# Sixteen modulation steps leave a ten-step recurrence for the input units ahead of it; scores are multiplied anew, three weight splits come after it

## The chip, the cores and the metric

The kernel runs on one core of one Trainium2 chip. The metric is the time of one execution in microseconds (us) on the device; lower is better. Engines are named as in the profile: PE (TensorE matmul), DVE (VectorE), ACT (ScalarE), POOL (GpSimd), SP (SyncE, which here only issues DMAs; its issue instructions are shown as SPq).

## The reference

The kernel computes one inference step of a two-layer backbone in fp32 for 128 context tokens and 512 latent tokens (640 in all, width 1024). Each layer is: half-step SwiGLU FFN, token mixing, half-step SwiGLU FFN. The even layer mixes by neighbourhood attention and by an mLSTM, the odd one by a gated short convolution.

```python
def modulation(cond, w, b):
    m = jax.nn.silu(cond) @ w + b
    return m.reshape(cond.shape[0], 1, N_MOD, D_MODEL)
def modulate_in(x, g_pre, mod, j):
    return rmsnorm(x, g_pre) * (1.0 + mod[:, :, 3 * j + 1]) + mod[:, :, 3 * j]
def gated_residual(x, out, g_post, mod, j, weight):
    return x + weight * mod[:, :, 3 * j + 2] * rmsnorm(out, g_post)
```

The change is about two parts of it. One is `modulation`: for each layer the two conditioning vectors times a 1024 x 9216 weight, that is 9 parts of 1024 columns. The other is the mLSTM of the even layer: 4 heads of width 128, in chunks of 128 tokens, two directions. Each of its 10 steps (5 chunks, 2 directions) takes scores (queries times keys), weights them by a decay, multiplies them with the values, adds the queries times the running memory C, and updates C.

## The kernel before, in words

The six sublayers (`SUBS`) run one after the other: ffn, ab (attention and mLSTM), ffn, ffn, sc (convolution), ffn. Every weight tile is loaded by SP into one of two slots `w_raw`, copied by ACT to `w_hi` (L1455), and DVE subtracts the copy to get `w_lo` (L2023); PE then multiplies hi by hi, lo by hi and hi by lo. Load n waits until tile n-2 is split.

**Modulation parts.** Most parts are summed by DVE from `ada_tile` rows (`mod_acc`, L2207 to L2209). Five parts (`DIRECT`, in sublayers 0, 1, 2, 3; sublayer 1 has two) go over PE instead: `load_direct` (L666) loads a 128x1024 piece of 512 KB into one of four slots `ada_direct`, and `direct_step` (L1086) multiplies it by the conditioning, 4 matmuls per piece (L1098) and 8 pieces per part, with 4 matmuls for the bias ahead of the first (L1096). `direct_out` (L1579) copies the sums to SBUF on ACT, `store_direct` (L688) stores them. SP issues all these loads and stores. In the FFN sublayers four steps stand behind unit 3 and four behind unit 5. The 16 steps of sublayer 1 stand inside the recurrence, two or three behind each of its steps 2 to 8 (`REC_AT`), with their loads between those of the output weight (`REC_LOADS`).

**The ab sublayer** has 23 input units (a 128-column tile of the input weight times all tokens, L1321, some 7.0 us each; unit 3 is a narrow one with the gates), with attention between the later ones. Then comes the recurrence: `products(q)` (L1337) multiplies the scores of step q, `back(q)` multiplies numerators (L1372, L1374) and the state's update (L1382). Around it, per step: POOL makes `q_scaled` (L1982), `v_weighted` (L1995) and a masked `decay` (L1973); ACT takes two exponentials (L1791, L1835); DVE makes `scoresT` (L2598) and finishes the step with denominators, `h_sum` and `C_state` (L2600 to L2629). Queries and keys of a chunk give the same product in both directions, so the scores of steps 0, 1, 2 are copied to SBUF by ACT (`keep_scores`, L1838) and used again in steps 7, 6, 5 (`SCORE_KEPT`). Splits of output weight tiles 1, 2, 3 stand on ACT and DVE behind steps 1, 3, 5.

**The output projection** of ab has 8 tiles of the contraction (15 matmuls of 128x512 each). Tiles 0 to 2 need only attention's output; then `turn_heads` transposes the normalised heads, and tiles 3 to 7 follow. SP's queue behind the recurrence: four stores of the final state, a wait for their landing (`st_out`), `load_gate`, output weight tiles 6 and 7, the stores of the two direct parts, the reload of x from DRAM (5 x 512 KB), the modulation columns of the next sublayer (`load_cols`), and the other weight loads.

## Time and profile before

| | |
|---|---|
| median of 3 runs | 2472.9 us (2469.79 to 2474.32) |
| the profiled execution | 2478.73 us, span 2476.8 us, mean granted clock 0.993 |
| ab sublayer: input units from | 502 us |
| the recurrence, first to last step on PE | 774.5 to 827.8 us |
| busy over the span | PE 98%, DVE 71%, ACT 40%, POOL 17% |

The span is that of one execution taken by the profiler. A row of the timeline gives the start, the duration, the engine, the line, the operation, the tile written and those read, and how many were joined (x4). What stands in brackets is how long the engine stood idle ahead of it and what it waited for. PE runs at one of two clock levels (1.2 and 2.4 GHz); a granted clock (PEclk) of 1.00 is the upper one. Matmuls overlap, so the distance between the starts of two rows tells more than their durations.

### The profile page before, as it was taken

How to read it: one execution, taken by the hardware profiler on the slowest of the kernel's cores; microseconds unless marked ns; L12 is line 12 of the kernel's file. 1: busy time of each engine (PE TensorE's matmuls, PEld its weight loads, DVE VectorE, ACT ScalarE, POOL GpSimd, SP SyncE). 2: the span in 40 equal slices, each digit the busy share in tenths (PEclk: the TensorE clock that was granted, in tenths of full speed). 3: DMA queues.
4: the chain of work that ended last, by engine and by line, in shares of the span. 5: the costliest groups of instructions: out<-in, count | busy, mean ns of one | idle time of the engine just before them, and what ended most of it. 6: DMA issues, size and time to landing. Idle time of an engine off the chain costs nothing. (4 is left out here: it accounts for less than half of the span.)

```text
span 2476.8 us, 39028 instructions
## 1 busy us (share of the span) xinstructions
PE 2416.2 (98%) x15205; PEld 2210.2 (89%) x15205; DVE 1747.8 (71%) x2449; ACT 983.4 (40%) x1924; POOL 411.8 (17%) x410
## 2 busy tenths in 40 slices
PE   6999999999998999999999999999999999999998
PEld 6997998889887789979988997999899979989997
DVE  5978785666555668778855988686567459866864
ACT  4442443532444454424435442343421154423432
POOL 1120220201214122102203220121200022201211
PEclk9999999999999999999999999999999999999999
DMA  8426334174124534263343426333244323243333
GB/s 260 129 61 219 100 87 139 54 232 111 46 58 164 186 112 131 80 207 86 86 162 112 124 72 209 98 86 115 90 145 137 103 85 103 69 149 99 86 110 112
DMA packets 346646, 297.95 MB, mean 120 GB/s; under 512 B 38219, under 2 KB 296251, under 8 KB 346464
## 3 DMA queue, kind: packets, MB, share of 16 engines
q1 hardware_dynamic: 346464, 295.46, 39.3%
q8 instruction: 122, 2.00, 0.3%
q14 instruction: 60, 0.49, 0.1%
HBM read 280.57 MB, written 14.80 MB: 119 GB/s over the span
## 5 line engine op out<-in xcount | busy, mean ns | idle before, releaser
L2023 DVE TENSOR_TENSOR w_lo<-w_raw,w_hi 128x512 fp32r<-128x512 f32 (+1 forms) x249 | 218.9, 882 | 254.7 <-ACT w_hi L1455 253.3
L1455 ACT ACTIVATE w_hi<-w_raw 128x512 fp32r<-128x512 f32 (+1 forms) x249 | 188.1, 760 | 473.7 <-DMA w_raw<-in_ffn_w_dram 205.5
L949 PE MATMUL psum<-w_hi,act_hi 128*128 128x512 f32 x800 | 319.0, 399 | 2.3 <-DVE w_lo L2023 2.1
L951 PE MATMUL psum<-w_hi,act_lo 128*128 128x512 f32 x800 | 317.1, 396 | 0.0
L950 PE MATMUL psum<-w_lo,act_hi 128*128 128x512 f32 x800 | 317.0, 396 | 0.0
L1082 PE MATMUL psum<-hT_hi,w_hi 128*128 128x320 f32 x912 | 281.9, 309 | 0.5 <-DVE z_quarters L2309 0.5
L1083 PE MATMUL psum<-hT_lo,w_hi 128*128 128x320 f32 x912 | 281.8, 309 | 0.0
L1084 PE MATMUL psum<-hT_hi,w_lo 128*128 128x320 f32 x912 | 281.8, 309 | 0.0
L949 PEld LDWEIGHTS psum<-w_hi,act_hi 128*128 128x128 f32 x800 | 150.6, 188 | 44.0 <-DVE w_lo L2023 5.5
L1082 PE MATMUL psum<-t_hi,w_hi_more 128*128 128x320 f32 x608 | 187.9, 309 | 0.0
L1084 PE MATMUL psum<-t_hi,w_lo_more 128*128 128x320 f32 x608 | 187.9, 309 | 0.0
L1083 PE MATMUL psum<-t_lo,w_hi_more 128*128 128x320 f32 x608 | 187.8, 309 | 0.0
L1932 POOL TENSOR_TENSOR w_sum<-w_raw 128x512 f32<-128x512 f32 x36 | 55.2, 1534 | 783.2 <-DVE w_lo L2271 783.2
L951 PEld LDWEIGHTS psum<-w_hi,act_lo 128*128 128x128 f32 x800 | 150.6, 188 | 36.6
L950 PEld LDWEIGHTS psum<-w_lo,act_hi 128*128 128x128 f32 x800 | 150.7, 188 | 35.4
L1082 PEld LDWEIGHTS psum<-hT_hi,w_hi 128*128 128x128 f32 x912 | 171.2, 188 | 0.7 <-DVE w_lo_more L2271 0.7
L1083 PEld LDWEIGHTS psum<-hT_lo,w_hi 128*128 128x128 f32 x912 | 171.2, 188 | 0.0
L1084 PEld LDWEIGHTS psum<-hT_hi,w_lo 128*128 128x128 f32 x912 | 171.2, 188 | 0.0
L1036 PE MATMUL psum<-hT_hi,w_hi 128*128 128x320 f32 x608 | 140.2, 312 | 2.4 <-DVE w_lo L2023 2.3
L1036 PE MATMUL psum<-hT_hi,w_lo 128*128 128x320 f32 x608 | 138.5, 309 | 0.0
L1036 PE MATMUL psum<-hT_lo,w_hi 128*128 128x320 f32 x608 | 138.4, 309 | 0.0
L2325 DVE TENSOR_TENSOR z_quarters<-z_quarters 128x640 f32<-128x640 f32 x76 | 127.4, 1676 | 4.8 <-ACT z_quarters L1624 4.8
(303 smaller groups left out, 5906.0 us busy)
## 6 DMA issues: line engine op xcount, KB each, us to landing
w_raw<-in_ffn_w_dram SPq DMA_DIRECT2D x96, 512.0 KB, 4.5
w_raw_next<-in_ffn_w_dram SPq DMA_DIRECT2D x80, 512.0 KB, 5.4
w_raw<-in_ffn_w_dram SPq DMA_DIRECT2D x148, 256.0 KB, 3.0
ada_tile_ffn<-in_ada_w_dram SPq DMA_DIRECT2D x56, 512.0 KB, 4.5
ada_direct<-in_ada_w_dram SPq DMA_DIRECT2D x40, 512.0 KB, 6.0
w_raw<-in_ab_w_in_dram SPq DMA_DIRECT2D x28, 512.0 KB, 4.3
w_raw<-in_sc_w_in_dram SPq DMA_DIRECT2D x24, 512.0 KB, 4.0
x_kept_rows<-x SPq DMA_DIRECT2D x20, 512.0 KB, 5.7
```

Of the source, the lines that this page charges most:

```text
L949: mm(out, a_hi, b_hi, start=first, stop=False)
L950: mm(out, a_hi, b_lo, start=False, stop=False)
L951: return mm(out, a_lo, b_hi, start=False, stop=final)
L1036: last = mm(IN[p][0:width, h, 0:HT], a, b[:, k, h * HT:(h + 1) * HT], start=(k == 0 and a is hi and b is hT_hi), stop=(k == KD - 1 and a i ...
L1082: mm(out, hi[:, k, :], o_hi[:, k, :], start=(k == 0 and q < 4), stop=False, **on)
L1083: mm(out, hi[:, k, :], o_lo[:, k, :], start=False, stop=False, **on)
L1084: last = mm(out, lo[:, k, :], o_hi[:, k, :], start=False, stop=(k == KH - 1), **on)
L1455: A(dst, src, ACT.Copy).then_inc(w_hi_ok, 1)
L1932: pool.tensor_tensor(S1[:], A21(g), A22(g), ALU.add).then_inc(ws_ok, 1)
L2023: V.tensor_tensor(d_, a, b.bitcast(F32), ALU.subtract).then_inc(w_lo_ok, 1)
L2325: V.tensor_tensor(Z[:, 2:4, :], Z[:, 0:2, :], Z[:, 2:4, :], ALU.mult).then_inc(q_summed, 1)
```

## The change

1. The 16 direct steps of sublayer 1 leave the recurrence: two stand behind each of the input units 3, 4, 5, 6, 8, 9, 10 and 11 (`AB_AT`), in PSUM bank 5. ACT copies the rows of the two parts behind units 7 and 11 (`AB_ROWS`) instead of behind the recurrence.
2. All loads and stores of direct parts, those of the FFN sublayers too, are issued by POOL instead of SP: in an FFN sublayer behind POOL's two `t_sum` additions, in ab at POOL's start.
3. `keep_scores` is gone; the scores of steps 5, 6 and 7 are multiplied anew (`SCORE_STEPS`), in alternating banks.
4. DVE splits the output weight tiles 1, 2, 3 behind the recurrence, between the scalings of heads; ACT's split of tile 3 comes behind it too.
5. The reload of x is issued behind input unit 15, and `load_cols` comes ahead of output weight tile 6.

```diff
-REC_AT = {2: (0, 2), 3: (2, 5), 4: (5, 8), 5: (8, 10), 6: (10, 12), 7: (12, 14), 8: (14, 16)}
-REC_LOADS = {3: (4, 8), 4: (8, 10), 5: (10, 16)}
+AB_AT = {u: range(2 * i, 2 * i + 2) for i, u in enumerate((3, 4, 5, 6, 8, 9, 10, 11))}
+AB_ROWS = {7: 0, 11: 1}
...
# SP
+                            if u == 15:
+                                direct_done(sp, s, 1, KD - 1)
+                                for t in range(NT):
+                                    reload_x(s, t)
...
-                        load_out(s, ab_w_out[0], 0, ph, 1, 3)
-                        for k in range(4):
-                            load_direct(s, 0, k)
-                        for u in range(3, AB_SPLIT):
-                            load_out(s, ab_w_out[0], 0, ph, u, u + 1)
-                            for j in range(*REC_LOADS[u]):
-                                load_direct(s, j // KD, j % KD)
+                        load_out(s, ab_w_out[0], 0, ph, 1, AB_SPLIT)
...
                         load_gate(s)
-                        load_out(s, ab_w_out[0], 0, ph, AB_SPLIT, AB_SPLIT + 2)
-                        for z in range(2):
-                            store_direct(s, z)
-                        for t in range(NT):
-                            reload_x(s, t)
-                        sp.wait_ge(mod_stored, STORED(DB[s] + 1))
                         load_cols(s + 1)
-                        load_out(s, ab_w_out[0], 0, ph, AB_SPLIT + 2)
+                        load_out(s, ab_w_out[0], 0, ph, AB_SPLIT)
...
# PE
                     modulation(ph, u)
+                    for j in AB_AT.get(u, ()):
+                        direct_step(1, j // KD, j % KD)
...
-                    if q in (2, 3):
+                    if q >= 2:
                         pe.wait_ge(ml_st, q - 1)
-                        pe.wait_ge(sc_kept, q - 1)
...
                     if q + 2 in SCORE_STEPS:
                         products(q + 2)
-                    if q == 2:
-                        pe.wait_ge(ml_st, 3)
-                        pe.wait_ge(sc_kept, 3)
-                    for j in range(*REC_AT.get(q, (0,))):
-                        direct_step(1, j // KD, j % KD)
...
# POOL, ffn
+                    for k in range(KD) if s in DIRECT else ():
+                        load_direct(s, 0, k)
...
# POOL, ab
+                    for j in range(2 * KD):
+                        load_direct(s, j // KD, j % KD)
+                        if j == KD + 3:
+                            store_direct(s, 0)
+                    store_direct(s, 1)
...
# DVE
-                    if q in (1, 3, 5):
-                        split(ph["nout"] + (q + 1) // 2, shape="out", u=(q + 1) // 2)
                 for n in range(2, NT):
+                    split(ph["nout"] + n - 1, shape="out", u=n - 1)
                     head_scale(n)
...
-SCORE_STEPS = [0, 1, 2, 3, 8]
-SCORE_BANK = {0: 0, 1: 1, 2: 0, 3: 1, 4: 1, 8: 1, 9: 1}
-SCORE_KEPT = {5: 2, 6: 1, 7: 0}
+SCORE_STEPS = [0, 1, 2, 3, 5, 6, 7, 8]
+SCORE_BANK = {0: 0, 1: 1, 2: 0, 3: 1, 4: 1, 5: 0, 6: 1, 7: 0, 8: 1, 9: 1}
```

Behind step 3 of the recurrence PE has this before: the state's update, three direct steps (pieces 2, 3 and 4 of the first part), the numerators of step 4.

```order
L1382 MATMUL psum<-v_weighted,km_tok 128x129 x3
L1098 MATMUL psum<-ada_direct_150,cond_silu 2x256 [waits direct_loaded2]
L1098 MATMUL psum<-ada_direct_150,cond_silu 2x256 x3
L1098 MATMUL psum<-ada_direct_151,cond_silu 2x256 [waits direct_loaded3]
L1098 MATMUL psum<-ada_direct_151,cond_silu 2x256 x3
L1098 MATMUL psum<-ada_direct_148,cond_silu 2x256 [waits direct_loaded0]
L1098 MATMUL psum<-ada_direct_148,cond_silu 2x256 x3
L1372 MATMUL psum<-vm_tok,scoresT 128x129 [waits ml_h,ml_cs,ml_qs,ml_st]
```

In the change four products of scores for step 5 stand there instead, and the bias with the first two steps now stands ahead of the narrow input unit with the gates (the unit's first matmul is the last row but one; it waits for its own split):

```order
L1054 MATMUL psum<-direct_bias_161,pick 2x256 [waits direct_loaded0]
L1054 MATMUL psum<-direct_bias_161,pick 2x256 x3
L1056 MATMUL psum<-ada_direct_148,cond_silu 2x256 x4
L1056 MATMUL psum<-ada_direct_149,cond_silu 2x256 [waits direct_loaded1]
L1056 MATMUL psum<-ada_direct_149,cond_silu 2x256 x3
L1280 MATMUL psum<-hT_hi,w_hi 16x320 [waits in_evac1,w_lo_ok]
L1280 MATMUL psum<-hT_hi,w_hi 16x320
```

So PE's queue now meets the landing of these pieces in the input units, and no longer in the recurrence.

At the end of the recurrence DVE has this before (the copy of the last state, three head scalings, the splits of tiles 4 and 5):

```order
L2628 COPY C_state<-psum 128x516 [waits ml_c]
L2637 TENSOR_TENSOR h_sum<-h_sum,h_r 128x512 [waits h_r_ok] x3
L2023 TENSOR_TENSOR w_lo<-w_raw,w_hi 128x512 [waits w_hi_ok] x2
```

and in the change (the splits of tiles 1, 2 and 3 between the scalings):

```order
L2609 COPY C_state<-psum 128x516 [waits ml_c]
L2006 TENSOR_TENSOR w_lo<-w_raw,w_hi 128x512 [waits w_hi_ok]
L2618 TENSOR_TENSOR h_sum<-h_sum,h_r 128x512 [waits h_r_ok]
L2006 TENSOR_TENSOR w_lo<-w_raw,w_hi 128x512 [waits w_hi_ok]
L2618 TENSOR_TENSOR h_sum<-h_sum,h_r 128x512 [waits h_r_ok]
L2006 TENSOR_TENSOR w_lo<-w_raw,w_hi 128x512 [waits w_hi_ok]
L2618 TENSOR_TENSOR h_sum<-h_sum,h_r 128x512 [waits h_r_ok]
L2006 TENSOR_TENSOR w_lo<-w_raw,w_hi 128x512 [waits w_hi_ok] x2
```

SP's queue in the change, from the loads of output tiles 3, 4 and 5 on (each waits for the split of the tile two before it):

```order
L594 DMA w_raw<-in_ab_w_out_dram 128x512 [waits w_lo_ok] x3
L594 DMA held_ab_raw_115<-in_ab_w_out_dram 128x512
L594 DMA w_raw<-in_ab_w_out_dram 128x512 [waits w_lo_ok]
L594 DMA held_ab_raw_118<-in_ab_w_out_dram 128x512
L594 DMA w_raw<-in_ab_w_out_dram 128x512 [waits w_lo_ok]
L594 DMA held_ab_raw_121<-in_ab_w_out_dram 128x512
L594 DMA out_dram<-C_state 128x4x128 [waits ml_cs]
L594 DMA out_dram<-C_state 128x4x1
L594 DMA out_dram<-C_state 128x4x128 [waits ml_cs]
L594 DMA out_dram<-C_state 128x4x1
L594 DMA gate<-modulation 128x2x1024 [waits direct_stored,mod_stored,x_new,ml_h,st_out]
```

The stores of the state stood behind the same loads before too, but those loads waited for splits inside the recurrence. POOL, in the third sublayer of the change:

```order
L1900 TENSOR_TENSOR t_sum_189<-hT_hi,hT_lo 128x1280
L1879 DMA direct_bias_162<-in_ada_b_dram 1x16x64 [waits xT_ok]
L1881 DMA ada_direct_152<-in_ada_w_dram 128x1024
L1881 DMA ada_direct_153<-in_ada_w_dram 128x1024 [waits xT_ok]
L1881 DMA ada_direct_154<-in_ada_w_dram 128x1024 [waits xT_ok]
L1881 DMA ada_direct_155<-in_ada_w_dram 128x1024 [waits xT_ok]
L1881 DMA ada_direct_152<-in_ada_w_dram 128x1024 [waits direct_used]
```

Before, SP issued these loads ahead of `t_sum`; now they follow it on POOL.

## Rows read from the trace of the kernel before

**Rows 1.** The page: busy time over the span

```profile
PE 2416.2 (98%) x15205; PEld 2210.2 (89%) x15205; DVE 1747.8 (71%) x2449; ACT 983.4 (40%) x1924; POOL 411.8 (17%) x410
```

**Rows 2.** Waits of PE, 771 to 862 us: in total, times, longest

```profile
PE psum L1098 <- DMA ada_direct<-in_ada_w_dram: 6.9, 4, 5.8
PE psum L1372 <- DVE scoresT L2598: 6.2, 2, 4.6
```

**Rows 3.** Timeline of PE in the recurrence (start us, us, engine, line, operation)

```profile
774.51 0.46 PE L1372 MATMUL psum<-vm_tok,scoresT 128*128 128x129 f32 x2 [1.56 <-DVE scoresT L2598]
...
777.27 1.06 PE L1351 MATMUL psum<-featT 128*128 128x128 f32 x8
...
778.16 0.39 PE L1372 MATMUL psum<-vm_tok,scoresT 128*128 128x129 f32 x2
...
782.70 0.46 PE L1372 MATMUL psum<-vm_tok,scoresT 128*128 128x129 f32 x2 [0.47 <-issue]
...
791.73 0.80 PE L1372 MATMUL psum<-vm_tok,scoresT 128*128 128x129 f32 x2 [4.60 <-DVE scoresT L2598]
...
815.99 1.03 PE L1098 MATMUL psum<-ada_direct,cond_silu 128*2 128x256 f32 x8 [5.76 <-DMA ada_direct<-in_ada_w_dram]
...
827.82 0.48 PE L949 MATMUL psum<-w_hi,mix_act 128*128 128x512 f32 x1
```

**Rows 4.** Timeline of DVE in the recurrence

```profile
783.72 7.35 DVE L2023 TENSOR_TENSOR w_lo<-w_raw,w_hi 128x512 fp32r<-128x512 f32 x1 [1.22 <-ACT w_hi L1455]
...
798.15 1.76 DVE L2598 TENSOR_TENSOR scoresT<-scores_kept,decay 128x512 f32<-128x512 f32 x1
```

**Rows 5.** Timeline of POOL in the recurrence

```profile
781.31 1.28 POOL L1982 TENSOR_TENSOR q_scaled<-featT,w_inter 128x512 f32<-128x512 f32 x1
...
784.79 1.28 POOL L1982 TENSOR_TENSOR q_scaled<-featT,w_inter 128x512 f32<-128x512 f32 x1
```

**Rows 6.** Busy time by engine in the recurrence (core 0: us, PE, PEld, DVE, ACT, POOL, PEclk, DMA)

```profile
771.00:828.00 57.00, 43.44 (x395) 34.21 (x394) 37.19 (x91) 29.60 (x108) 33.87 (x32) 0.91 0.65 221
```

**Rows 7.** Timeline of SP behind the recurrence

```profile
826.35 4.37 SPq L606 DMA_DIRECT2D out_dram<-C_state  x4
...
838.87 0.37 SPq L606 DMA_DIRECT2D gate<-modulation  x1
...
839.79 0.43 SPq L606 DMA_DIRECT2D w_raw<-in_ab_w_out_dram  x1
```

**Rows 8.** Timeline of ACT, output tile 6

```profile
846.15 0.63 ACT L1455 ACTIVATE w_hi<-w_raw 128x512 fp32r<-128x512 f32 x1 [10.09 <-DMA w_raw<-in_ab_w_out_dram]
```

**Rows 9.** Timeline of DVE, output tile 6

```profile
850.62 0.69 DVE L2023 TENSOR_TENSOR w_lo<-w_raw,w_hi 128x512 fp32r<-128x512 f32 x1
```

**Rows 10.** Timeline of PE, output tile 6

```profile
851.38 0.50 PE L949 MATMUL psum<-w_hi,mix_act 128*128 128x512 f32 x1
```

**Rows 11.** Timeline of PE in the ab input units

```profile
519.62 0.46 PE L1321 MATMUL psum<-hT_hi,w_hi 128*16 128x320 f32 x2 [2.44 <-DVE w_lo L2023]
...
591.38 1.89 PE L1117 MATMUL psum<-mod_acc_ab,pick 128*2 128x256 f32 x16 [3.75 <-DVE mod_acc_ab L2209]
...
594.43 0.73 PE L1321 MATMUL psum<-hT_hi,w_lo 128*128 128x320 f32 x2
```

**Rows 12.** A stretch of the ab input units (columns as in Rows 6, then GB/s)

```profile
515.00:525.00 10.00, 7.56 (x52) 5.44 (x52) 9.30 (x10) 1.88 (x4) 0.00 (x0) 1.00 1.00 301
```

**Rows 13.** Timeline of POOL, third sublayer

```profile
913.74 6.16 POOL L1926 TENSOR_TENSOR t_sum<-hT_hi,hT_lo 128x1280 f32<-128x1280 f32 x2 [15.32 <-DVE w_lo L2023]
```

**Rows 14.** Timeline of PE, third sublayer

```profile
929.01 0.61 PE L1096 MATMUL psum<-direct_bias,pick 1*2 1x256 f32 x8
...
929.54 1.91 PE L1098 MATMUL psum<-ada_direct,cond_silu 128*2 128x256 f32 x32
```

**Rows 15.** A stretch of the third sublayer (columns as in Rows 6)

```profile
920.00:930.00 10.00, 10.00 (x81) 8.91 (x83) 9.93 (x8) 5.36 (x6) 0.00 (x0) 1.00 0.19 55
```

**Rows 16.** The page: DMA issues, median us to landing

```profile
ada_direct<-in_ada_w_dram SPq DMA_DIRECT2D x40, 512.0 KB, 6.0
```

More of the change, by code:

```diff
@@ L14 @@
-import itertools
 from contextlib import ExitStack, contextmanager
@@ L343, in build @@
             [where["silu_g"], where["u_tmp"], a3] + [hh + i * 2048 for i in range(5)] + [hl + i * 2048 for i in range(2)])]
-        Sk = [at(f"scores_kept{i}", [P, MLH, P], hl + 4096 + i * 2048) for i in range(3)]
         hssq = at("h_ssq", [P, NT * MLH], hl + half + 8192 + 480)
@@ L461, in build @@
             ph[-1]["mods_end"] = mb
-            if s == 1:
-                DB[s], mb = mb, mb + len(DIRECT[s])
         parts = [(s, z) for s in DIRECT for z in range(len(DIRECT[s]))]
-        direct_parts = [DB[s] + z for s, z in parts]
-        bias_until = list(itertools.accumulate(16 if b in direct_parts else 64 for b in range(mb)))
         held_use = lambda s, i: (1 if i < NT else 0) + sum(1 for q in range(s + 1) if plan[q][-1]["held"] > i)
@@ L733, in load_pairs @@
                         keep_x(s, t)
-                    for k in DIRECT_LOADS.get(2 * i + 1, ()) if s in DIRECT else ():
-                        load_direct(s, 0, k)
                 for g in range(ph["g0"], ph["g1"]):
@@ L1098, in direct_step @@
                     last = mm(out(i), csil[:, :, k], direct[s][k % 4][:, cols(i)], start=False, stop=(k == KD - 1))
-                last.then_inc(mod_mm if k == KD - 1 else direct_used, 1)
+                last.then_inc(direct_used, 1)
             def modulation(ph, u):
@@ L1174, in out_phase @@
                         turns({3: (0, 1), 4: (2,), 5: (3,)}[k])
-                    for t in ((0, 1, NT - 1, 2, 3) if ph.get("ab") and k == 0 else range(NT)):
+                    for t in ((NT - 1, 0, 1, 2, 3) if ph.get("ab") and k == 0 else range(NT)):
                         if k == 0:
@@ L1856, in mixing @@
                     if n == NT - 1:
-                        direct_out(1, 0)
-                        direct_out(1, 1)
+                        split(ph["nout"] + 3, shape="out", u=3)
                     head_squares(n)
```

138 lines of the change are left out of this document (65 added, 73 removed).

## The prediction, made before the change had run

> **What bounds the kernel now.** The page first: PE is busy 98% of the span [rows 1], so almost every microsecond that PE is spared or kept waiting counts, and work of other engines is free as long as PE does not wait for it. Then I looked for PE's waits around the recurrence [rows 2]: 6.9 us for the landing of direct pieces and 6.2 us for `scoresT`. The timeline of PE shows where they are [rows 3]. The recurrence runs from 774.51 to 827.82, that is 53.3 us for ten steps. Its second step begins 3.65 us after its first, and that is what a step of PE costs with numerators, state update and four score products (the products are the 0.9 us from 777.27 to 778.16). Ten such steps would be 36 us. What lies between is three things: 16 direct steps; an idle of 4.60 us ahead of step 3, and one of 5.76 us ahead of a direct step; and the lower clock level after them, since the granted clock is 0.91 over the stretch [rows 6].
>
> The first idle is not a lack of DVE time. DVE's split of an output tile, which takes 0.69 us elsewhere [rows 9], took 7.35 us there, and `scoresT` stood behind it [rows 4]. POOL worked back to back in this time, starting a scaled query every 3.48 us [rows 5]. So a DVE instruction with two SBUF operands was held for as long as POOL kept going; a `scoresT` that reads `scores_kept` from SBUF was stretched as well, to 1.76 us [rows 4]. The Trainium skill, "SBUF — State Buffer", section "Who interferes with whom", says that a DVE operation with two SBUF inputs and a GpSimd operation that reads SBUF exclude each other for one whole instruction. The trace agrees on the direction and not on the size, as 7.35 us is several POOL instructions of 1.28 us and not one.
>
> **(a) The recurrence without direct steps, splits and kept scores.** It removes 16 steps, both idles and both clock drops, and adds three groups of products at 0.9 us. POOL sets the pace at first: step 2 can begin no earlier than before, 782.70, because its scaled query ends at 782.59 [rows 3, 5]. Step 3 follows 3.48 us later (784.79 + 1.28 us, 786.2 with the signal). From there PE's own 3.65 us is the longer period: steps 4, 5 and 6 begin at 789.8, 793.4 and 797.0. DVE is no bound: of its 37.19 us over the stretch [rows 6] some 9.4 are splits, so 2.8 us a step. Steps 6 and 7 have no state update (2.7 and 1.8 us); 8 and 9 alternate with DVE at about 2.5 us each. The end comes at 806.6 instead of 827.82: **-21.2 us, I take -21**. If POOL and DVE alternate less well it is -19.5; I see no way past -21.5. The three copies of scores taken from ACT save nothing by themselves.
>
> **(b) The 16 steps in the input units.** A step is 1.91 / 4 = 0.48 us by the row and 0.46 by the starts, a bias 0.53 [rows 14]. The first two steps and their bias (1.5 us) stand ahead of the gates' unit, where PE idles 2.44 us anyway for a split that waits behind `mod_acc` on DVE [rows 11]. They fit into the gap, but they must have landed, and in this stretch the 16 DMA engines are busy all the time (share 1.00, 301 GB/s) [rows 12] with the weight and `ada_tile` loads on which that split depends: 2 MB more at 301 GB/s is 7 us of such traffic. Between nothing and 7 us I take +1.9 for the gates' unit and +1 for later landings. The other 14 steps and the second bias are 14 x 0.46 + 0.53 = 7.0, with 0.1 for each change between streams 7.7. Against it stands the wait of 3.75 us at 591.38 for a `mod_acc` [rows 11]. The work that leads to it starts from the turned context gates, behind unit 9; only the four steps of units 10 and 11 come into the wait and fill it, -1.9. With 1.9 us of idle left the clock should stay up, as it did at the 2.44 us idle [rows 11, 12], and the stretch after 591.38, where a pair of 128x320 matmuls takes 0.73 instead of 0.46 us [rows 11], goes: -2.4 over some 5 us. ACT's row copies, moved into its idle time behind units 7 and 11, cost nothing; POOL has no work before unit 13. Sum 1.9 + 1 + 7.7 - 1.9 - 2.4: **+6.3**, between +3.5 (no late landing) and +10 (late tiles and the clock drop kept).
>
> **(c) The tail.** Let T be the start of the output projection (827.82 before). SP must issue the loads of tiles 3, 4, 5 and then four stores; it waits for their landing, and only then come gate, columns and tile 6. Before, the stores were issued from 826.35 to 830.72, T+2.9 at the last; the gate went out at T+11.05, so 8.15 us for landing [rows 7]. Now load 3 waits for the split of tile 1, which DVE makes after its last state copy at T+1.9; load 5 waits for the split of tile 3, which waits for load 3 to land: T+8.3. The stores go at T+9.1 to T+11.1 and have landed at T+19.3. Gate, g_post and three column loads take 2.2 us, so load 6 is issued at T+21.5. Before, ACT's copy of tile 6 began 6.36 us after its load [rows 7, 8] and took 0.63 us; add DVE's 0.69 and tile 6 is ready at T+29.2. PE came to it at T+23.56 without a wait, just after the split's end at 851.31 [rows 9, 10]. So **a new wait of +5.7 us**, and as after the idles of 3.75 to 5.76 us above, a stretch at the lower level, +1.7: **+7.4**, between 0 (stores landing in 3 us because nothing else is under way, loads too) and +10 (the head scalings, between which the splits now stand, late as well). The direct rows' stores and the reload of x, which leave this place, were hidden there behind other work and give nothing.
>
> **(d) The FFN sublayers.** POOL ends `t_sum` at 919.90 [rows 13] and PE wants the bias at 929.01 [rows 14]: 9.1 us for five issues and a landing. No row of this trace shows a DMA issued by POOL. From below: SP's issues, 0.43 us for a weight tile [rows 7], which with the 6.0 us of a landing [rows 16] give 8.2 us, no wait. From above: POOL is held like DVE was in [rows 4], DVE being busy 9.93 of 10 us here [rows 15]; five issues at 2 us plus a landing are 16 us, minus 9.1, less the 1.9 us that PE spends on the bias and the pieces ahead of the last: 5 us, three times. I take the lower end with a little, 0.3 us each, **+1**, because the DMA engines have room (share 0.19) [rows 15] and `t_sum` itself ran at its usual pace beside the same DVE work (3.1 us for 1280 columns [rows 13] against 1.28 for 512 [rows 5]). For the other four pieces PE is a unit pair later, and they have time.
> The Trainium skill, "DMA: Bandwidth & Descriptors", section "Anatomy of one DMA — SWDGE (gpsimd) path", gives 2.0 us plus bytes / 436e3 for a DMA issued by GpSimd; my estimate from it for one piece is 3.2 us, and that would leave no wait in (d).
>
> **Sum:** -21 + 6.3 + 7.4 + 1 = -6.3 us. Against the profiled execution, 2478.7, that is 2472.4; that execution lies 5.8 us above the median of 2472.9, so the forecast of the median is 2466.6, rounded **2467 us**.
>
> **The rivals.** A measurement of this kernel can tell 0.2%, 4.9 us, from no change: below 2468.0 is faster, above 2477.8 slower.
> *POOL's loads come late (the other side).* Mechanism: in three FFN sublayers, five issues of POOL, one after the other beside a busy DVE, last longer than the room behind `t_sum`. It decides from the point where an issue costs over about 1 us (5 x 1 + 6.0 - 1.9 = 9.1). At 2 us PE waits 4.5 to 5 us three times, with lower clock after it: +14 in place of +1, so **2480**. For it: DVE's 7.35 us shows that the two engines can hold each other for long, and DVE is never idle there. Against: `t_sum` is not stretched.
> The same section of "SBUF — State Buffer" in the Trainium skill has a warning by a box on DMAs of GpSimd, that DVE's two-port work starves the writing of their descriptors, 620 ns becoming 3100 ns; no run here shows it yet.
> *Late pieces in ab.* The 8 MB in input units land behind the weights in a stretch at share 1.00, and (b) is +12: **2473**, no change. For it: a piece took 6.0 us to land already where the engines were less busy [rows 6, 16]. Against: the pieces behind the first four are asked for a unit or more before their use.
> *The recurrence stays slow.* If the long hold of DVE came from POOL's pace and hits another operation, `h_sum` or `C_state` with their SBUF operands, 7 us come back: **2474**. Against: both read PSUM as well, and the two stretched instructions read SBUF alone [rows 4].
> *The tail has no new wait.* Stores that land in 3 to 4 us because the traffic of the direct pieces is gone take (c) to 0: **2459**.
>
> **How the numbers follow.** The forecast 0.45; POOL's loads late 0.15; late pieces in ab 0.15; recurrence slow 0.10; no wait in the tail 0.15. The forecast's own range, from its bounds, is 2461 to 2473, of which 0.32 of the 0.45 lies below 2468.0. Faster: 0.32 + 0.15 and a little of the others, 0.50. Same: the rest of the forecast, the two cases at 2473 and 2474, 0.33. Slower: POOL's loads and a part of late pieces, 0.17. The range 2459 to 2479 leaves out most of the 0.15 of the first rival and the far end of the last.
>
> **What would show it.** The recurrence on PE shorter by 21 us, with no idle over 1.6 us and no clock drop; in the units, PE 7 to 10 us more between unit 3 and the recurrence and the wait for `mod_acc` under 2.4 us; in the tail, a wait of 5 to 6 us for the split of tile 6, and the gate issued some 19 us behind T; in sublayers 0, 2 and 3 the bias matmul waiting under 1 us. The forecast is wrong if PE waits for `ada_direct` by several us in any sublayer, if a step of the recurrence takes over 4 us, or if tile 6 is not waited for.

## The result, and the profile after

| | before | changed |
|---|---|---|
| median (20 runs each, the same chip) | 2471.64 us | 2476.42 us |
| lowest to highest | 2468.05 to 2477.3 us | 2472.71 to 2481.76 us |
| the profiled execution | 2478.73 us | 2474.26 us |

The ratio is 1.0017, with an interval of 1.0011 to 1.0023: the changed kernel is slower by 4.2 us. That is under the 0.2% that the prediction took as its bound, so the verdict is "same". The forecast was 2467, 5 us faster; the direction was wrong, and the time lies inside the range. Note the third line: the profiled execution of the changed kernel is 4.5 us *shorter* than that of before. What a reader of these two traces alone would conclude is the opposite of what the medians say, and a part of this study is about that.

The page of the changed kernel:

```profile
span 2472.5 us, 39072 instructions
PE 2414.1 (98%) x15229; PEld 2208.0 (89%) x15229; DVE 1739.1 (70%) x2449; ACT 983.5 (40%) x1921; POOL 444.1 (18%) x475
q0 software_dynamic: 6560, 21.04, 2.3%
ada_direct<-in_ada_w_dram POOLq DMA_DIRECT2D x40, 512.0 KB, 6.0
```

Nothing here tells where time went. POOL's queue now carries the 40 pieces, and they land as fast as before, 6.0 us in the median [rows 16].

**The recurrence** did what was asked of it. PE's timeline from its first step to the output projection:

```profile
785.10 0.46 PE L1330 MATMUL psum<-vm_tok,scoresT 128*128 128x129 f32 x2 [1.56 <-DVE scoresT L2579]
...
788.75 0.39 PE L1330 MATMUL psum<-vm_tok,scoresT 128*128 128x129 f32 x2
...
793.27 0.46 PE L1330 MATMUL psum<-vm_tok,scoresT 128*128 128x129 f32 x2 [0.46 <-issue]
...
817.36 0.48 PE L906 MATMUL psum<-w_hi,mix_act 128*128 128x512 f32 x1
```

From 785.10 to 817.36 it takes 32.26 us, against 53.31 [rows 3]: 21.05 us less, where 21 was forecast. Over this stretch the clock is up throughout, where it was 0.91 [rows 6]:

```profile
785.00:817.36 32.36, 29.84 (x257) 29.00 (x257) 25.13 (x83) 23.04 (x90) 31.37 (x32) 1.00 0.20 59
```

**The input units** are where it is given back. PE's waits between 483 and 785 us:

```profile
PE psum L1280 <- DVE w_lo L2006: 4.7, 2, 4.5
PE psum L1192 <- DVE probs L2451: 1.9, 1, 1.9
PE psum L1075 <- DVE mod_acc_ab L2194: 0.2, 1, 0.2
```

The wait for `mod_acc` that was 3.75 us [rows 11] is down to 0.2. But the gates' unit waits 4.51 us instead of 2.44 for its split, and there is a wait for `probs` that before did not have:

```profile
521.52 0.71 PE L1280 MATMUL psum<-hT_hi,w_hi 128*16 128x320 f32 x2 [4.51 <-DVE w_lo L2006]
...
628.80 0.55 PE L1192 MATMUL psum<-ident,probs 128*128 128x128 f32 x3 [1.92 <-DVE probs L2451]
```

The first of these durations is already the lower clock level at work (0.71 us, 0.46 in the kernel before [rows 11]). On DVE, the multiplication by the conditioning ahead of the gates' split stood 9.15 us for a load of `ada_tile`, where it had stood 5.54. Before, then changed:

```profile
515.37 1.42 DVE L2207 TENSOR_SCALAR mod_acc_ab<-ada_tile_ab,cond_silu 128x1024 f32<-128x1024 f32 x2 [5.54 <-DMA ada_tile_ab<-in_ada_w_dram]
...
517.27 1.42 DVE L2192 TENSOR_SCALAR mod_acc_ab<-ada_tile_ab,cond_silu 128x1024 f32<-128x1024 f32 x2 [9.15 <-DMA ada_tile_ab<-in_ada_w_dram]
```

The stretches there (us, then busy time of PE, PEld, DVE, ACT, POOL, then granted clock, DMA share and GB/s) show traffic in place of work, and the clock going down behind the wait:

```profile
505.00:515.00 10.00, 9.79 (x67) 9.53 (x66) 1.23 (x1) 1.89 (x4) 1.93 (x4) 1.00 0.99 307
515.00:525.00 10.00, 5.49 (x42) 2.52 (x41) 6.58 (x7) 2.08 (x5) 1.23 (x2) 0.78 1.05 383
525.00:535.00 10.00, 10.00 (x71) 6.71 (x70) 9.06 (x8) 1.64 (x2) 1.07 (x2) 0.88 1.04 281
```

A second execution of before has in the first two of them:

```profile
505.00:515.00 10.00, 9.62 (x66) 9.35 (x65) 1.23 (x1) 2.20 (x5) 0.00 (x0) 1.00 0.78 176
515.00:525.00 10.00, 7.52 (x52) 5.30 (x51) 8.24 (x9) 1.89 (x4) 0.00 (x0) 1.00 1.06 328
```

The four pieces asked for at POOL's start, from 504.76 us on, raise the traffic of the first stretch to 307 GB/s, from 176 here and 200 and 186 in the first and third executions of before. The loads that the gates' split hangs on land later; that the pieces are the cause is tested below (thin pieces).

**The tail** has the wait that was forecast. SP behind the recurrence, and then the ACT, DVE and PE rows of output tile 6:

```profile
825.67 2.44 SPq L594 DMA_DIRECT2D out_dram<-C_state  x4
837.51 0.37 SPq L594 DMA_DIRECT2D gate<-modulation  x1
...
840.17 0.44 SPq L594 DMA_DIRECT2D w_raw<-in_ab_w_out_dram  x1
```

```profile
845.22 0.63 ACT L1408 ACTIVATE w_hi<-w_raw 128x512 fp32r<-128x512 f32 x1 [15.28 <-DMA w_raw<-in_ab_w_out_dram]
845.88 0.69 DVE L2006 TENSOR_TENSOR w_lo<-w_raw,w_hi 128x512 fp32r<-128x512 f32 x1 [5.20 <-ACT w_hi L1408]
846.63 0.79 PE L906 MATMUL psum<-w_hi,mix_act 128*128 128x512 f32 x1 [5.34 <-DVE w_lo L2006]
```

**The FFN sublayers** show no wait: POOL issues its loads in 0.54 us each, and PE has no wait for a piece or a bias in any of them. In the third:

```profile
914.07 0.65 POOL L1879 DMA_DIRECT2D direct_bias<-in_ada_b_dram  x1
914.72 2.14 POOL L1881 DMA_DIRECT2D ada_direct<-in_ada_w_dram  x4
```

The two traces by stage, from the starts of the same PE rows, in us. The marks are the first product of input unit 0 (484.25 us before; the 502 us given ahead of the prediction is the start of unit 2), the first step of the recurrence, the output projection, output tile 6, and the transposes of the last of five token tiles of the new x. The last mark stands 7 to 10 us into the third sublayer's first products, so that what PE loses around them is counted in "ab".

| | input units | recurrence | to tile 6 | to the end of ab | ab |
|---|---|---|---|---|---|
| before | 290.3 | 53.3 | 23.6 | 53.0 | 420.1 |
| changed | 302.1 | 32.3 | 29.3 | 52.0 | 415.6 |

That is +11.8, -21.1, +5.7, -1.0: ab is 4.5 us shorter, and so are the profiled executions. The medians differ by 4.8 us the other way.

One statement ahead of the prediction needs mending: the narrow input unit with the gates is unit 4, counted from 0, not unit 3. The first two direct steps stand behind unit 3, ahead of it.

### The profile page after: what moved, and what is told of

The parts are those of the page before. It is cut to its first block and busy times, and to the rows that moved or that the text cites. A ratio compares the mean times of both kernels' runs of the same rounds, so it can differ in the third digit from the quotient of the medians.

```text
span 2472.5 us, 39072 instructions
## 1 busy us (share of the span) xinstructions
PE 2414.1 (98%) x15229; PEld 2208.0 (89%) x15229; DVE 1739.1 (70%) x2449; ACT 983.5 (40%) x1921; POOL 444.1 (18%) x475
## 5 line engine op out<-in xcount | busy, mean ns | idle before, releaser
L2006 DVE TENSOR_TENSOR w_lo<-w_raw,w_hi 128x512 fp32r<-128x512 f32 (+1 forms) x249 | 211.2, 851 | 270.0 <-ACT w_hi L1408 269.1
```

Source lines behind the costliest of these rows:

```text
L2006: V.tensor_tensor(d_, a, b.bitcast(F32), ALU.subtract).then_inc(w_lo_ok, 1)
```

## The experiments

Medians are in us; each ratio is to before, with its 95% interval, from runs of before on the same chip. Edits are made on the changed kernel, but for the last one, which is made on before.

**Both kernels again, unchanged.** Two more pairs were wanted to see what in the two traces is the kernel's and what is one execution's.

> The kernel before, unchanged. Theory 1: its first profiled execution (2478.7 us, above all its 20 timed runs) was an unlucky one, with a wait of 5.8 us for a direct piece, one of 4.6 us for scoresT and three drops of the clock. Another execution lies near 2471.6 us and its trace shows a recurrence of some 46 to 50 us instead of 53.3, or a drop of the clock less at 895 us. Rival: the execution looks as before, 53 us in the recurrence, and its place in time differs for reasons outside of these stretches. Ratio to the kernel before: 1.000.

> The changed kernel, unchanged. Theory 1: ratio 1.0017 (+4 us), recurrence 32.3 us, wait for output tile 6 of 5.3 us, input units 10 to 12 us longer than before, as in its first trace; of these the input units vary most, since their pieces compete with the weights. Rival: recurrence or tail vary by more than 1 us.

> The kernel before, a third profiled execution. Theory 1 (the 53.3 us of the first trace was the long end): recurrence of 47 to 51 us, split in the recurrence of 1 to 2 us and not 7.35, waits for direct pieces 5 to 9 us in sum. Rival: 53 us again. Input units 290 us in both.

> The changed kernel, a third profiled execution. If profiled executions of the changed kernel lie below its median by more than chance, this one does too, by 1 to 3 us, and its ab sublayer is 416 us from the first input unit to the end of the projection as in the other two. If it was chance, it is as likely above. Recurrence 32.3 us, input units 301 to 302 us.

| | median | ratio | profiled execution | units | recurrence | to tile 6 | to the end | ab |
|---|---|---|---|---|---|---|---|---|
| before again | 2474.29 | 1.0003 (0.9992 to 1.0014) | 2479.12 | 290.1 | 48.8 | 23.6 | 51.1 | 413.6 |
| before, third | 2474.57 | 0.9999 (0.9988 to 1.0010) | 2477.83 | 291.3 | 49.9 | 23.6 | 51.6 | 416.3 |
| changed again | 2480.39 | 1.0024 (1.0013 to 1.0035) | 2478.28 | 301.6 | 32.3 | 30.1 | 52.1 | 416.0 |
| changed, third | 2478.63 | 1.0026 (1.0017 to 1.0035) | 2479.92 | 303.9 | 32.3 | 29.6 | 52.4 | 418.1 |

Four things follow. First, the changed kernel is slower in each comparison, by 0.17, 0.24 and 0.26%. Second, its recurrence takes 32.3 us every time, while before's takes 53.3, 48.8 and 49.9 (the expected 46 to 50 for the second was right). The split of 7.35 us [rows 4] did not come back; the same split, then the product that reads kept scores, in the second execution of before:

```profile
783.57 1.65 DVE L2023 TENSOR_TENSOR w_lo<-w_raw,w_hi 128x512 fp32r<-128x512 f32 x1 [1.24 <-ACT w_hi L1455]
...
792.53 1.76 DVE L2598 TENSOR_TENSOR scoresT<-scores_kept,decay 128x512 f32<-128x512 f32 x1
```

What does come back each time is the wait for direct pieces, here 1.74 and 4.17 us ahead of two steps, and 5.9 us for the longest in the third execution. PE's timeline of the second and PE's waits of the third, from 774 to 862 us:

```profile
792.55 0.61 PE L1098 MATMUL psum<-ada_direct,cond_silu 128*2 128x256 f32 x8 [1.74 <-DMA ada_direct<-in_ada_w_dram]
...
810.07 0.62 PE L1098 MATMUL psum<-ada_direct,cond_silu 128*2 128x256 f32 x8 [4.17 <-DMA ada_direct<-in_ada_w_dram]
```

```profile
PE psum L1098 <- DMA ada_direct<-in_ada_w_dram: 9.0, 4, 5.9
```

Third, the means of three are -18.4 in the recurrence, +11.9 in the units, +6.1 to tile 6 and +0.3 behind it: in the traces ab comes out even (-0.1), outside ab nothing differs in a set way, and still the medians say +5.5. The gap sits in how the profiled executions lie to the medians: those of before lie 7.1, 4.8 and 3.3 us above the median of their own runs, those of the changed kernel -2.2, -2.1 and +1.3. The means are +5.1 and -1.0, 6 us apart, which is the gap.

Fourth, where before's excess sits is not settled. The first execution spends 4 us more in the recurrence than the other two. But the expectation that the second would lie near 2471.6 us was missed: its ab is 6.5 us shorter than the first's, and it is as long (2479.12 and 2478.73 us), because outside ab it takes 2063.6 us of its span against 2056.7. So single executions of one kernel scatter outside ab by more than the effect.

**Splits back in the recurrence.**

```diff
# ACT
-                    if q in (1, 3):
+                    if q in (1, 3, 5):
                         split(ph["nout"] + (q + 1) // 2, shape="out", u=(q + 1) // 2)
...
# DVE
+                    if q in (1, 3, 5):
+                        split(ph["nout"] + (q + 1) // 2, shape="out", u=(q + 1) // 2)
...
-                    split(ph["nout"] + n - 1, shape="out", u=n - 1)
```

> The changed kernel with the splits of output tiles 1, 2, 3 on DVE and ACT back inside the recurrence, behind steps 1, 3 and 5. Theory 1 (POOL working back to back holds a DVE instruction with two SBUF operands): one split takes 5 us or more and the recurrence gets 4 to 8 us longer, with a clock drop behind it; in return the loads of tiles 3 to 5 and the stores go out early and the wait for tile 6 (5.3 us and 1.7 us of lower clock) is gone: same time as the changed kernel within 3 us. Rival (the hold was an accident of one execution): splits of 0.7 to 1.3 us, recurrence 33 us, 7 us less than the changed kernel.

Measured: 2473.18, ratio 0.9998 (0.9986 to 1.0010); by the ratios some 6 us less than the changed kernel, where the rival had 7. The recurrence is 33.9 us, 1.6 longer, the way to tile 6 is 23.7, as before: the wait in the tail is gone. With direct steps out of the recurrence, splits inside it cost 0.88, 0.68 and 1.65 us, in DVE's timeline:

```profile
797.25 0.88 DVE L2004 TENSOR_TENSOR w_lo<-w_raw,w_hi 128x512 fp32r<-128x512 f32 x1 [0.76 <-ACT w_hi L1408]
...
812.80 1.65 DVE L2004 TENSOR_TENSOR w_lo<-w_raw,w_hi 128x512 fp32r<-128x512 f32 x1
```

The stores go out right behind the recurrence (the output projection starts at 822.36), and the gate 11.6 us behind that start, against 20.2 us in the changed kernel; PE's row of tile 6 has no wait:

```profile
821.36 4.37 SPq L594 DMA_DIRECT2D out_dram<-C_state  x4
...
833.95 0.37 SPq L594 DMA_DIRECT2D gate<-modulation  x1
```

```profile
846.07 0.48 PE L906 MATMUL psum<-w_hi,mix_act 128*128 128x512 f32 x1
```

So the split of three tiles behind the recurrence buys 1.6 us there and costs 5.9 us here.

**Stores ahead of the last load.**

```diff
-                        load_out(s, ab_w_out[0], 0, ph, 1, AB_SPLIT)
+                        load_out(s, ab_w_out[0], 0, ph, 1, 4)
...
+                        load_out(s, ab_w_out[0], 0, ph, 4, AB_SPLIT)
```

The four stores of the final state stand between the two.

> The changed kernel with one edit: the four stores of the final state are issued behind the load of output tile 3 and ahead of the loads of tiles 4 and 5. Theory 1 (the tail's wait hangs on when the stores land): the gate goes out some 4.5 us earlier, load 6 with it, PE's wait for tile 6 shrinks from 5.3 us to about 1 us and the clock does not drop: 6 us less than the changed kernel, ratio to the kernel before 0.9993. Rival (the landing of the stores is slow because of weight loads ahead of it, or load 6 is late for another reason): wait still over 3 us, ratio 1.001 or more.

Measured: 2481.26, ratio 1.0031 (1.0018 to 1.0043), a miss. The gate went out 19.6 us behind the projection's start instead of 20.2 and not 4.5 us earlier, and the wait moved forward and grew. PE, SP and ACT:

```profile
842.83 1.08 PE L1362 MATMUL psum<-ident,h_sum 128*128 128x128 f32 x4 [8.62 <-DVEq L2646]
```

```profile
822.14 3.12 SPq L594 DMA_DIRECT2D out_dram<-C_state  x4
825.30 1.12 SPq L594 DMA_DIRECT2D w_raw<-in_ab_w_out_dram  x1
```

```profile
838.01 0.63 ACT L1408 ACTIVATE w_hi<-w_raw 128x512 fp32r<-128x512 f32 x1 [7.90 <-DMA w_raw<-in_ab_w_out_dram]
```

The load of tile 4, issued behind the stores, was copied by ACT 12.7 us after its issue; DVE's split of it stands ahead of the last scalings of heads, and PE waited 8.6 us for those instead of 5.3 for tile 6. A split in an engine's program is a place where everything behind it waits for a DMA.

**Kept scores back** (on top of splits back): `keep_scores`, its semaphore and `SCORE_KEPT` as in the kernel before.

```diff
-SCORE_STEPS = [0, 1, 2, 3, 5, 6, 7, 8]
+SCORE_STEPS = [0, 1, 2, 3, 8]
+SCORE_KEPT = {5: 2, 6: 1, 7: 0}
```

> The changed kernel with the splits back in the recurrence and, in addition, the scores of steps 0 to 2 kept in SBUF by ACT and used again in steps 5 to 7, as in the kernel before (no scores multiplied anew). Theory 1 (the scores make no difference to the end of the recurrence by themselves: PE saves 3 x 0.9 us, but DVE's scoresT then reads two SBUF operands and is held beside POOL): recurrence 32 to 35 us, within 1.5 us of the 33.9 us with scores multiplied anew; two of three scoresT from kept scores take over 1.2 us. Rival (multiplying anew is a real cost on PE's path): recurrence 31.5 us or less and the kernel 2 us or more faster.

Measured: 2477.39, ratio 1.0010 (1.0001 to 1.0019), against 0.9998 for splits back alone. By the ratios it is 3 us slower, but the two intervals overlap, so the medians do not show it; the traces do for the recurrence. Neither expectation was met. The recurrence takes 37.2 us instead of 33.9, and PE's waits for `scoresT` grow from 2.5 to 6.5 us in total, the longest from 1.6 to 2.4:

```profile
PE psum L1335 <- DVE scoresT L2594: 6.5, 4, 2.4
```

```profile
805.01 1.75 DVE L2594 TENSOR_TENSOR scoresT<-scores_kept,decay 128x512 f32<-128x512 f32 x1
```

The three products that read kept scores take 1.75, 1.32 and 1.53 us where those that read PSUM take 0.68. Multiplying the scores anew, at 0.9 us of PE, gives the shorter recurrence once no direct step is in it.

**Direct steps one unit later.**

```diff
-AB_AT = {u: range(2 * i, 2 * i + 2) for i, u in enumerate((3, 4, 5, 6, 8, 9, 10, 11))}
+AB_AT = {u: range(2 * i, 2 * i + 2) for i, u in enumerate((4, 5, 6, 7, 8, 9, 10, 11))}
...
+                    pool.wait_ge(w_lo_ok, plan[s][0]["nin"] + 4)
```

The wait stands ahead of POOL's first load.

> The changed kernel with the direct steps of the ab sublayer one unit later: two behind each of units 4 to 11, and POOL issues the first load only once the gates' tile (unit 3) is split. Theory 1 (the 2 MB of the first four pieces land in a stretch where the DMA engines are full and delay ada_tile and with it the split of the gates' tile): PE's wait for the gates' unit falls from 4.2 to 4.5 us to the 2.4 us of the kernel before and the clock does not drop there; the input units get 4 to 6 us shorter, 296 to 298 us instead of 302. Rival (the two steps and their bias cost as much wherever they stand, or the pieces come too late for unit 4): input units 300 us or more, a wait for ada_direct.

Measured: 2478.31, ratio 1.0019 (1.0010 to 1.0028). The experiment missed its aim by one split: the wait let POOL go at 511.26 us, still ahead of the gates' unit, and that waited 4.46 us as in the changed kernel. The unit starts 37.4 us behind unit 0, against 38.4 to 38.8 in the three traces of the changed kernel and 34.7 to 35.4 in before's. So moving the two steps and the first loads gave back 1.2 us of 3.5; this run does not tell the steps from the loads. The units take 300.1 us, where the expectation had 296 to 298. That is 2.4 less than the changed kernel's mean, but stores early and splits back, which have its units unchanged, took 300.0 and 302.5.

**Loads later still.** The same with six units from unit 5 on and `nin + 5`.

```diff
+AB_AT = {5: range(0, 2), 6: range(2, 5), 7: range(5, 8), 8: range(8, 11), 9: range(11, 14), 10: range(14, 16)}
...
+                    pool.wait_ge(w_lo_ok, plan[s][0]["nin"] + 5)
```

> The changed kernel with the first direct loads of the ab sublayer issued only when the gates' tile is split (the run before let them go one split too early, while ada_tile was still landing), and with the 16 steps behind units 5 to 10, two or three each. Theory 1: PE's wait ahead of the gates is 2.4 us as in the kernel before and the clock stays up: gates' unit starts 35.3 us after the first unit, input units 3 to 6 us shorter than the changed kernel's 302, ratio 1.000 or 1.001. Rival: the wait stays over 4 us, or the traffic only moves the lateness to the weights of units 5 to 8 and the sum stays at 301 to 302 us.

Measured: 2480.82, ratio 1.0026 (1.0015 to 1.0037). Now the gates' unit waits 2.61 us with the clock up, as before; but the 16 pieces come in a denser row behind it, and a wait with a clock drop appears two units on:

```profile
519.10 0.46 PE L1280 MATMUL psum<-hT_hi,w_hi 128*16 128x320 f32 x2 [2.61 <-DVE w_lo L2007]
...
536.84 0.56 PE L1280 MATMUL psum<-hT_hi,w_hi 128*128 128x320 f32 x2 [2.03 <-DVE w_lo L2007]
```

The wait for `probs` is there as well (2.1 us). The units take 301.5 us against 302.5 in the mean: the lateness moved, it did not go, as the rival had it.

**The reload of x back in the tail.**

```diff
-                            if u == 15:
-                                direct_done(sp, s, 1, KD - 1)
-                                for t in range(NT):
-                                    reload_x(s, t)
...
+                        load_out(s, ab_w_out[0], 0, ph, AB_SPLIT, AB_SPLIT + 2)
+                        for t in range(NT):
+                            reload_x(s, t)
+                        load_out(s, ab_w_out[0], 0, ph, AB_SPLIT + 2)
```

> The changed kernel with the reload of x (5 x 512 KB) issued behind output tile 7 in the output phase, as before, instead of behind input unit 15. Theory 1 (the reload stands ahead of the input unit's weight load in SP's queue and in the DMA engines; ACT copies that weight 3.7 us late, DVE's split with it, and attention's probs behind the split): the wait of 1.5 to 2.2 us for probs near 629 us and its clock drop go, 3 to 5 us in the input units; nothing is lost in the tail. Rival (the wait has another cause, such as POOL's later bias additions): the wait stays and the input units are unchanged within 1 us.

Measured: 2479.33, ratio 1.0023 (1.0014 to 1.0032): no gain by itself. But the units take 298.7 us and the wait for `probs` is gone, and the reason is in SP's queue. In the changed kernel:

```profile
610.80 2.54 SPq L594 DMA_DIRECT2D x<-x_kept_rows  x5
613.38 7.06 SPq L594 DMA_DIRECT2D bias_raw<-bias_rep  x16
620.49 1.26 SPq L594 DMA_DIRECT2D w_raw<-in_ab_w_in_dram  x2
```

and with the reload late:

```profile
615.03 5.50 SPq L594 DMA_DIRECT2D bias_raw<-bias_rep  x16
620.57 1.26 SPq L594 DMA_DIRECT2D w_raw<-in_ab_w_in_dram  x2
```

By ACT's copy of a feature tile in the same unit (620.16 and 622.57 us), the weight load goes out 0.3 us behind it in the first and 2.0 us ahead of it in the second. ACT's copy of that weight, DVE's split and the softmax sums behind it all follow, and PE waits for their end. The size varies: the nine traces with the reload behind unit 15 have a wait for `probs` there of 0.3 to 2.3 us, the seven with the reload in the tail have none. In this execution some 4 us came back at 890 us, where the clock was 0.67 and 0.65 for 10 us. Six of the other 15 traces have a lower level between 880 and 905 us too (0.50 to 0.95 in two or three stretches of 5 us), the first and third of before among them, the rest not. It goes with no edit, so I read nothing into it, and the medians leave open whether the reload alone gains.

**Three repairs together** (splits back, steps one unit later, reload late), and the same with the later loads in place of the later steps.

> The changed kernel with three edits together: splits of output tiles 1 to 3 back in the recurrence, direct steps one unit later with late first loads, reload of x in the output phase. Theory 1: the gains add: 7 us (splits) and 4 to 6 us and 3 to 5 us, so 14 to 18 us under the changed kernel, 2462 to 2466 us, ratio to the kernel before 0.995 to 0.9965. Rival (they cover each other, or the reload in the tail now delays tiles 6 and 7): ratio 0.998 or more.

> Splits back in the recurrence, reload of x in the output phase, and the later loads and steps of the run above. Theory 1: 3 to 5 us under the version with the same first two edits and the loads one split earlier: 2466 to 2468 us, ratio to the kernel before 0.9965 to 0.9975. Rival: no gain over it, ratio 0.998 to 0.999.

Measured: 2471.04, ratio 0.9984 (0.9975 to 0.9993), and 2470.42, ratio 0.9986 (0.9977 to 0.9995). Both are faster than both kernels; against the changed one, by the ratios, that is some 8 to 10 us. Both expectations were missed (0.995 to 0.9965, and 0.9965 to 0.9975); the rivals, that the gains cover each other, were right. Their units take 299.6 and 296.8 us, their recurrences 33.8. Most of the gain is that of splits back alone (0.9998); what the other two repairs add, some 3 us, is not clear of the intervals.

**Thin pieces.** Of each direct piece of sublayer 1 only the first 64 of 1024 columns are loaded (32 KB instead of 512), and the matmuls read these again and again, so that PE does the same number of columns. Modulation parts 7 and 8 of layer 1 are therefore left out. First on the changed kernel, then on **before**:

```diff
+                    pool.dma_start(direct[s][k % 4][:, 0:64], src[:, 0:64]).then_inc(direct_loaded[k % 4], 16)
...
+                        last = mm(out(i).rearrange("p (a b) -> p a b", a=4), csil[:, :, k], direct[s][k % 4][:, None, 0:64].to_broadcast([P, 4, 64]), start=False, stop=(k == KD - 1))
```

> The changed kernel, where the 16 direct pieces of the ab sublayer are loaded only to 64 of their 1024 columns and these 64 are multiplied 16 times over: the modulation parts 7 and 8 of the first layer are left out, PE's time for them stays and 15/16 of their 8 MB of traffic go. Theory 1 (competition for the DMA engines is what made the input units 12 us longer instead of 6): the gates' unit starts 35 to 36 us after the first unit as before, its wait is 1 us or less above the steps' 1.5 us, no clock drop there, input units 296 to 298 us. Rival (PE's own time and the order of waits make the 12 us): 300 us or more, and a wait of over 4 us ahead of the gates with its clock drop.

> The kernel before, where the 16 direct pieces of the ab sublayer are loaded only to 64 of 1024 columns and multiplied 16 times over (modulation parts 7 and 8 of the first layer left out), still inside the recurrence. Theory 1 (of the 51 us of the recurrence some 8 us are waits for these pieces and 2 to 3 us the lower clock after them, in every execution and not only in the profiled ones): recurrence 39 to 42 us, and 8 to 11 us less in the medians, ratio to the kernel before 0.9955 to 0.997. Theory 2 (the waits are large in the profiled executions, which lay 3 to 6 us above the medians of the kernel before, and small in the others): the trace shows the same 8 to 11 us, the medians 4 to 6 us, ratio 0.9975 to 0.9985.

Measured, on the changed kernel: 2473.10, ratio 0.9998 (0.9987 to 1.0008). The units take 295.0 us, so of their 11.9 us more, 7.5 go with the traffic of 8 MB and 4.4 stay: PE's own 7.7 us less the waits that went. The gates' unit waits 0.72 us with the clock up; the wait for `probs` is 1.1 us, so a part of the reload's cost goes with the traffic too. On before: 2468.46, ratio 0.9983 (0.9973 to 0.9993), 4.2 us faster, while by the traces its ab is 10.3 us shorter than before's mean (recurrence 42.6 us, one wait of 3.8 left). Here the trace overstates by 6 us as well, though this one execution lies 3.1 us below the median of its own runs, which is half of that:

```profile
805.74 1.05 PE L1102 MATMUL psum<-ada_direct,cond_silu 128*2 128x256 f32 x16 [3.81 <-DMA ada_direct<-in_ada_w_dram]
```

This bears on the gap, but does not close it. The expectation's second theory, that the waits for landings are larger in the profiled executions of before than in its others, forecast a ratio of 0.9975 to 0.9985 and got 0.9983. It is not shown by that: half of the 6 us is this execution's own place, and the second execution of before has its excess outside ab. A rival is chance. The profiled executions of the ten variants, none of which but this one has direct steps in the recurrence, lie from 4.3 us below their medians (direct steps one unit later) to 4.3 above (splits back). Three of before at +5.1 in the mean would be unusual in that scatter, but three are few. The cause is open, and the size is rough.

## Why the prediction was wrong, by its own steps

**(a) The recurrence: right as a mechanism, 3 us too large as a difference of kernels.** -21 was worked out, -21.05 measured between the first two traces, and the ways (POOL's pace first, then PE's 3.65 us, no idle over 1.6 us, no clock drop) are in the rows. One step did take over 4 us, 788.75 to 793.27, which the prediction named as a sign of being wrong; but it was the one that its own working had put at 4.54, from 778.16 to 782.70 [rows 3]. But 53.3 us was the slowest of three executions of before; the mean gain by traces is 18.4. The hold of 7.35 us, to which the prediction gave a paragraph, was 1.65 us in the next execution.

**The step that failed: "that execution lies 5.8 us above the median of 2472.9, so the forecast of the median is 2466.6".** Against the profiled execution the sum was near, 2472.4 forecast and 2474.3 measured. It was then carried over to the medians as if the changed kernel's executions would stand 5.8 us above their median too. They stand 2.2 and 2.1 below it and 1.3 above. The prediction gave no reason for the carrying over. Had the 5.8 been left with the kernel before, the forecast would have been 2472: no change. There was a sign of it: one execution 4 us above the highest of three timed runs, with two idles of 4.6 and 5.8 us in the very stretch to be changed. That the step failed is shown; that the excess sat in these waits is not: the first execution spent 4 us more in the recurrence than the other two, but these lie 4.8 and 3.3 us above their medians all the same.

**(b) The units: mis-sized, +6.3 forecast, +11.9 measured, beyond the upper bound of +10.** PE's part was nearly right: 7.7 less 1.9 and 2.4 for the `mod_acc` wait and the clock behind it is +3.4, and thin pieces leave +4.4. The wait fell further than forecast, from 3.75 to 0.2 us. The traffic was put at 1.9 + 1 us and costs 7.5. Two terms failed. At the gates' unit about 2 us more of idle was to be all; the idle came as forecast, 4.51 instead of 2.44, but the clock dropped at it in all three traces of the changed kernel, and in one of three of before. "With 1.9 us of idle left the clock should stay up" was said of the `mod_acc` wait, of which only 0.2 was left; as a rule it does not hold, since the clock fell behind idles of 1.92, 2.03 and 2.06 us. And the reload of x was costed at nothing for where it left; where it went, ahead of a weight load in SP's queue, it makes a new wait of 1.9 us. It was weighed at its old place only. The rival "late pieces in ab" named the +12 but not the mechanism: the pieces were never late, as its "against" had it; the weights and `ada_tile` rows that they displaced were.

**(c) The tail: right.** Tile 6 ready at T+29.2 by the working; PE took it at T+29.27. The wait is 5.34 us (5.7 forecast), the stage and its clock +6.4 in the mean (7.4 forecast). The gate went out at T+20.2, 19.3 forecast. Splits back removes it whole.

**(d) The FFN sublayers: right, and less still.** No wait. POOL's issue costs 0.54 us, below the 1 us from which the rival "POOL's loads come late" would decide, while DVE is as busy there as before (9.90 of 10 us from 920 on, 9.93 before [rows 15]). Of the Trainium skill's warning in "SBUF — State Buffer", that DVE's work through both ports delays the descriptors of a GpSimd DMA, 620 ns becoming 3100, no run here is a test: 40 issues landed in 6.0 us in the median, and DVE's instructions beside those of the FFN sublayers were TENSOR_TENSORs but for one CAST in each. The page gives the two times for a `tensor_copy`, in its section "A bandwidth-pool intuition that's wrong (but worth ruling out)" and not in the one that the prediction names.

**The sum,** by the means of three traces: -6.3 forecast, plus 2.6 (a), plus 5.6 (b), minus 1.0 (c), minus 1 (d), is -0.1, and ab comes out at -0.1. The step from there to the medians, +5.5, is the failed one. With the executions of before 5.1 us above their median and those of the changed kernel 1.0 below, it is worth 6 us.

The rival "the recurrence stays slow" fell (32.3 us three times), and so did "the tail has no new wait".

The change is thus a trade: by the traces 18.4 us gained in the recurrence, 11.9 paid in the units and 6.4 in the tail. If the gap of 6 us belongs to the recurrence, which is not shown, the gain is 12 to 13 in the medians. The two payments are not tied to the gain. Splits back saves the tail's, the two variants with all repairs some of the units' too, and only with these is the whole clear of no change, at 0.14 to 0.16%.

## What to carry to other kernels

When the profiled execution lies above every timed run, do not shift the sum by the excess unless you can say where it sits, and look for it in the stretch that you mean to change first; one more execution of the kernel before would have shown that a hold of 7 us was a chance. A transfer that is moved is paid at its new place: in the issues of the queue (2.5 us for five reloads ahead of a weight load) and in the traffic of that stretch (8 MB where the DMA engines were already at 0.8 to 1.0 cost 7.5 us, though no piece itself was ever late). And an operand that DVE reads from PSUM can be cheaper than a kept copy in SBUF while POOL works: here 0.9 us of PE bought 0.6 to 1.1 us of DVE on the path, and the recurrence was 3.3 us shorter; the medians do not settle it.

## What was not expected of the hardware

- The length of an idle did not decide whether the clock fell. In the input units it fell at or just behind idles of 1.92, 2.03, 2.06, 2.13 and 2.49 us and stayed up behind idles of 2.44, 2.48 and 2.61 us. The first three executions of before had 2.44, 2.48 and 2.06 us ahead of the gates' unit, and only the third, with the shortest, lost the clock (granted 0.66, third execution of before):

```profile
520.00:525.00 5.00, 4.27 (x19) 2.44 (x20) 4.14 (x5) 1.06 (x1) 0.00 (x0) 0.66 0.92 295
```

- In seven of the 16 traces the lower level came with no PE idle above 0.43 us in the 60 us ahead of it. Each time it began within 1.1 us of the end of the same 2.3 us of PE's program, 28 small products of the gates (4x4 to 4x10 elements each). In the other nine traces the same 28 products had no such drop. So they are a suspect and not a shown cause. The second variant with all repairs, PE 5.00 of 5.00 us busy, granted clock 0.66:

```profile
595.00:600.00 5.00, 5.00 (x25) 4.98 (x25) 4.90 (x6) 0.00 (x0) 1.21 (x1) 0.66 0.50 122
```

- A DVE instruction that reads two operands from SBUF beside a busy POOL takes up to 1.8 us instead of 0.68, and rarely much more. In eight traces with three splits each in the recurrence, 23 splits took 0.68 to 1.81 us and one 7.35.
- The profiled executions of before were above the median of their runs all three times, those of the changed kernel once in three, and those of the ten variants four times.
